# Values last in each attention visit, and gates behind the biases

## The chip, the cores and the metric

The kernel runs on one core of a Trainium2 chip. TensorE multiplies, VectorE (DVE), ScalarE (ACT) and GpSimd (POOL) work elementwise, SyncE (SP) issues most transfers; each engine runs its own instructions in order, and engines meet only through semaphores. The metric is the device time of one execution in microseconds, as a median over runs.

## The reference

One inference step of a hybrid backbone in f32: two layers over 1024 latent and 128 context tokens, width 1024. Every layer normalises, makes one input projection, feeds four mixers of 256 channels, multiplies each by its own gate path, and projects back:

```
h, gate = modulate(x, c, g, w_mod, b_mod)          # RMSNorm, scale and shift
parts = split_proj(h @ w_in)                       # 3584 columns
ya, yb = chunk_mlp(...) * silu(az), short_conv(...) * silu(bz)
yc = window_attn(cq, ck, cv, kc, vc, sink) * silu(cz)
yd = neighbourhood_attn(dq, dk, dv, kd, vd, rpb) * silu(dz)
x = x + gate * (concatenate([ya, yb, yc, yd]) @ w_out)
```

Both attention mixers have four heads of 64 channels. In C a block of 128 queries sees the blocks on both sides, itself and 128 cached keys; in D an 8 by 16 tile of the 16 by 64 grid sees 12 x 32 grid keys and the 128 cached ones, with a bias table. A block of context tokens sees only context tokens. Softmax over the keys, then the product with the values.

## The kernel before

**The stream of TensorE.** The input projection is 28 tiles of 128 columns, each in three chunks of 384 tokens. A chunk is one *step* (`STEPS`, 84 in a layer, numbered g from 0): 8 blocks of the inner dimension by three matmuls of 128x384 (high by high, high by low, low by high halves), 24 in all, at L919. Between steps TensorE pays a *visit* to the attention. A fixed table sets what it holds: a *pair* is two heads of one mixer for one block of 128 queries, 36 pairs in a layer, numbered p.

- `S_AT`: the **scores** of pair p (L939, two heads, contraction over 64 channels, so 64-row pieces of the array) in steps 12 to 29 (pairs 0 to 17), 31 to 39 and 43 to 51. SCALE and signs are folded in elsewhere.
- `T_AT` = that step + 2: the **turned probabilities** (L949), transposes of up to 4 blocks for each head by a product with the identity, 128x128.
- `V_AT` = that step + 3: the **values** product (L961), 64 output channels a head, so 64-column pieces of the array, into psum bank `BANK_O`, columns 0 to 127.

So a full visit of step g holds values of the pair of step g-3, turns of g-2 and scores of g, in this order. In the middle of a chunk (ahead of block k = 4) `misc(g)` puts in small pieces that use `BANK_O`, columns 128 up: turned values (L969), the mixing products of mixer A (L978), and for the modulation vectors `mod_sums` (L987, steps 15 and 16) and `mod_turn` (L995, steps 17 and 18). misc waits until all values issued so far have been gated; values of step g wait through `misc_free(g)` until the piece of step g has been read out of the bank.

**VectorE's step g**: gate of the pair whose values TensorE makes in this step (`gate_pair`, L1366, waits for `values_ready`); `take_part` (L1244: reads a z tile's chunk out of psum, frees its bank); for the scores of this step two `bias_unit` (sink copy L1335, and L1343, which adds a bias and takes the minimum); then rope (`ROPE_AT`: steps 6, 9, 15; L1222, L1224, L1227, with one product on GpSimd, L665), parts of the modulation sums (`multiply`, L1185, steps 6 to 13), two `norm_unit` (L1350, L1353, wait for the exponents), and `mods_at(g + 1)`, which reads the modulation piece of the next step's misc (copy L1198 for steps 15 and 16, L1207 for 17 and 18).

**ScalarE's step g**: takes or tanh of the chunk; `copy_probs` (L830) of the turned probabilities of this step, which waits until the values of the pair before are done, since it overwrites the buffer they read; the high half of the weights (L695) every third step; two exponents (L821), which wait for the biases; and the copy of the next step's turned values.

Of the kernel before, what the change touches and what calls it, by code (L numbers as in the profile page):

```python
# [96 lines left out]
GROUP_P = LT + 1  # L97
# [14 lines left out]
def build(nc, xT, cond, w_mod, b_mod, norm_g, final_g, w_tiles, w_sT, b_s, w_conv, sink, rpb,  # L112
          cckT, ccv, cdkT, cdv, ident_c, rope_c, band_c, row_c, col_c, yT, sckT, scvT, sdkT, sdvT):
    with ExitStack() as ctx:
# [411 lines left out]
        for layer in range(DEPTH):  # L526
          with nc.Block() as block:
# [383 lines left out]
            def _(pe):  # L911
# [41 lines left out]
                def values(p):  # L953

                    u = 2 * p
                    pe.wait_ge(copied, u + 2)
                    if p >= 1:
                        pe.wait_ge(gated, p)
                    for b in range(BLOCKS[u]):
                        for r in range(2):  # L960
                            last = nc.tensor.matmul(psum[64 * r:64 * r + 64, BANK_O, 0:P], unit_values(u + r)[b],  # L961
                                                    probT[:, r, b * P:(b + 1) * P], start=(b == 0),
                                                    stop=(b == BLOCKS[u] - 1), skip_group_check=True)
                    last.then_inc(values_ready, 1)
# [91 lines left out]
                for g, (n, c) in enumerate(STEPS):  # L1056
                    if c == 0:
                        pe.wait_ge(lo_ready, n + 1)
                    if n == 1 and c == 0:
                        pe.wait_ge(rstd_copied, NCH)  # L1060
                    if n >= 2:
                        pe.wait_ge(free[c], n - 1)
                    for k in order:
                        if k == 4:
                            misc(g)
                        if n == 0:
                            pe.wait_ge(h_odd if k % 2 else h_even, 4 * c + k // 2 + 1)
                        last = products(n, k, c, order)
                    last.then_inc(chunk_done, 1)

                    if g in V_AT:
                        p = V_AT[g]
                        if p == 0:
                            pe.wait_ge(cv_natural, 3)
                        misc_free(g)
                        if p == 2 * GROUP_P:
                            pe.wait_ge(cache0_in, 16)
                            pe.wait_ge(dv_natural, 6)
                        if p == 3 * GROUP_P:
                            pe.wait_ge(cache1_in, 16)  # L1080
                            pe.wait_ge(dv_natural, 12)
                        values(p)
                    if g in T_AT:
                        turn_probs(2 * T_AT[g])
                        turn_probs(2 * T_AT[g] + 1)
                    if g in S_AT:
                        p = S_AT[g]
                        if p == 0:
                            pe.wait_ge(layer_in, 16 * LAYER_IN)
                            pe.wait_ge(rope_ready, 2)  # L1090
                        if p == GROUP_P:
                            pe.wait_ge(rope_ready, 3)
                        if p == 2 * GROUP_P:
                            part_read(pe, NO["dk", 0])
                            for b in range(NCH):
                                part_read(pe, NO["dq", 0], b)
                        if p == 3 * GROUP_P:
                            part_read(pe, NO["dk", 1])
                            for b in range(NCH):
                                part_read(pe, NO["dq", 1], b)  # L1100
                        scores(p)

                order = Y_ORDER
                for f in range(KT):
# [21 lines left out]
            def _(dve):  # L1126
# [248 lines left out]
                                                ALU.subtract).then_inc(y_low_v, 1)  # L1375

                for g, (n, c) in enumerate(STEPS):
                    if g in V_AT:
                        gate_pair(V_AT[g])
                    take_part(n, c)  # L1380
                    if g in S_AT:
                        p = S_AT[g]
                        if p == 0:
                            dve.wait_ge(layer_in, 16 * LAYER_IN)
                            settle()
                            tell(nc.vector.tensor_scalar(sinks[:, :], sinks[:, :], -1.0, None, ALU.mult))
                            settle()
                        bias_unit(2 * p)
                        bias_unit(2 * p + 1)
                    if g in ROPE_AT:  # L1390
                        rope(ROPE_AT[g])
                    if g in MOD_AT:
                        multiply(MOD_AT.index(g))
                    if 52 <= g < 56:
                        normalise(g - 52)
                    if g in S_AT:
                        norm_unit(2 * S_AT[g])
                        norm_unit(2 * S_AT[g] + 1)
                    mods_at(g + 1)
                    if g + 1 in MIX_AT:  # L1400
                        read_mix(MIX_AT[g + 1])
                    if g >= OUT_0 - 3:
                        y_low(g - (OUT_0 - 3))
# [183 lines left out]
```

## Time and profile before

| | |
|---|---|
| median of 3 runs | 1307.63 us (1305.5 to 1308.05) |
| profiled execution, its own time | 1307.76 us |
| its span, first to last instruction | 1305.9 us |
| mean granted clock of TensorE | 0.964 |
| TensorE busy | 1205.3 us, 92% |
| VectorE, ScalarE, GpSimd busy | 50%, 33%, 26% |

Matmuls overlap in the pipeline, so the starts of the rows are a better measure than their durations: projection matmuls start 0.17 us apart and are listed with 0.33. In a timeline a group of like instructions in a row stands as one row with its count; one f32 matmul of values or scores is two records there, one turn is one. The granted clock is 1.00 at 2.4 GHz and 0.50 at 1.2 GHz.

### The profile page before, as it was taken

The page shows a single profiled execution, that of the slowest core. Times are in us where ns is not written, and L with a number is a line of the kernel's source. Part 1 is how long each engine was busy: PE and PEld are TensorE (multiplying, and loading weights), DVE is VectorE, ACT ScalarE, POOL GpSimd, SP SyncE. Part 2 cuts the span into 40 slices and gives each one's busy share as a digit, 9 for nine tenths or more (in the row PEclk, how much of TensorE's full clock was granted, in tenths as well). Part 3 has the DMA queues.
Part 4 walks back from the last instruction along what each step waited for, and adds up shares of the span by engine and source line. Part 5 has one row for each costly group of instructions (what it writes and reads, how often), then busy time and mean ns, then how long its engine had stood idle before and what let it go on. Part 6 is the DMA issues. An engine that isn't in the chain of part 4 may idle for free. (4 is left out here: it accounts for less than half of the span.)

```text
span 1305.9 us, 19971 instructions
## 1 busy us (share of the span) xinstructions
PE 1205.3 (92%) x8010; PEld 1109.7 (85%) x8010; DVE 648.1 (50%) x1310; ACT 430.2 (33%) x908; POOL 338.5 (26%) x222
## 2 busy tenths in 40 slices
PE   2589799999999999999958889999999999999993
PEld 0389698988888999999958878898888899999993
DVE  3667744444254532397667674444424444225225
ACT  3351344545354111221136233544434411123110
POOL 0243131034250212341123313102424112134110
PEclk9799999999999999999969999999999999999997
DMA  8714111021120111345342421102112000121213
GB/s 346 275 57 158 38 43 36 17 66 55 57 70 17 33 49 33 133 138 177 101 177 93 127 70 41 38 17 66 56 46 80 19 33 33 49 101 43 95 53 145
DMA packets 35948, 107.12 MB, mean 82 GB/s; under 512 B 5264, under 2 KB 14608, under 8 KB 34576
## 3 DMA queue, kind: packets, MB, share of 16 engines
q1 hardware_dynamic: 34128, 105.06, 23.1%
q8 instruction: 64, 1.05, 0.3%
q10 hardware_dynamic: 1728, 0.79, 0.2%
q14 instruction: 28, 0.23, 0.1%
HBM read 90.88 MB, written 14.94 MB: 81 GB/s over the span
## 5 line engine op out<-in xcount | busy, mean ns | idle before, releaser
L919 PE MATMUL psum<-h_hi,w_hi 128*128 128x384 f32 x1728 | 599.6, 347 | 35.5 <-POOL h_lo L653 16.4
L919 PE MATMUL psum<-h_hi,w_lo 128*128 128x384 f32 x1728 | 582.8, 337 | 0.0
L919 PE MATMUL psum<-h_lo,w_hi 128*128 128x384 f32 x1728 | 582.5, 337 | 0.0
L919 PEld LDWEIGHTS psum<-h_hi,w_hi 128*128 128x128 f32 x1728 | 327.7, 190 | 69.8 <-issue 23.7
L633 POOL TENSOR_TENSOR w_lo<-w_raw,w_hi 128x1024 fp32r<-128x1024 f32 x72 | 180.7, 2510 | 722.8 <-ACT w_hi L695 722.8
L919 PEld LDWEIGHTS psum<-h_lo,w_hi 128*128 128x128 f32 x1728 | 328.0, 190 | 0.0
L919 PEld LDWEIGHTS psum<-h_hi,w_lo 128*128 128x128 f32 x1728 | 327.5, 190 | 0.0
L695 ACT CAST w_hi<-w_raw 128x1024 fp32r<-128x1024 f32 x72 | 75.8, 1053 | 243.3 <-PE psum L919 234.5
L821 ACT ACTIVATE prob<-prob,stat 128x512 f32<-128x512 f32 (+2 forms) x144 | 96.8, 674 | 87.9 <-DVE stat L1343 87.5
L1366 DVE SCALAR_TENSOR_TENSOR xy<-psum,xy 128x128 f32<-128x128 f32 x72 | 21.0, 292 | 175.9 <-PE psum L961 175.9
L1353 DVE TENSOR_SCALAR prob<-prob,stat 128x512 f32<-128x512 f32 (+1 forms) x144 | 103.0, 715 | 8.8
L830 ACT COPY probT<-psum 128x512 f32<-128x512 f32 (+1 forms) x144 | 70.8, 543 | 77.8 <-PE psum L949 77.7
L1185 DVE SCALAR_TENSOR_TENSOR slots<-slots,silu 128x1024 f32<-128x1024 f32 x56 | 82.7, 1517 | 4.2 <-DMA slots<-in_w_mod 1.7
L961 PE MATMUL psum<-probT,slots 128*64 128x128 f32 x896 | 71.1, 285 | 11.5 <-DVE slots L1198 8.3
L961 PEld LDWEIGHTS psum<-probT,slots 128*64 128x64 f32 x896 | 49.5, 138 | 29.7 <-issue 20.3
L1343 DVE CUSTOM_DVE_ANT_0 prob<-psum,table 128x512 f32<-128x512 f32 (+1 forms) x72 | 43.7, 645 | 61.6 <-PE psum L939 61.6
L643 POOL TENSOR_TENSOR table<-row_mask,table 128x384 f32<-128x384 f32 x48 | 40.4, 841 | 129.6 <-DMA table<-in_rpb 129.5
L949 PE MATMUL psum<-ident,prob 128*128 128x128 f32 x512 | 73.1, 284 | 0.0
L1422 DVE SCALAR_TENSOR_TENSOR xy<-psum,mod,slots 128x384 f32<-128x384 f32 (+1 forms) x64 | 31.6, 514 | 81.2 <-PE psum L919 79.5
L782 ACT ACTIVATE slots<-psum 128x384 f32<-128x384 f32 x60 | 28.7, 488 | 119.4 <-PE psum L919 119.4
L949 PEld LDWEIGHTS psum<-ident,prob 128*128 128x128 f32 x512 | 56.7, 144 | 11.8 <-issue 11.6
L811 ACT ACTIVATE slots<-psum 128x384 f32<-128x384 f32 x48 | 23.6, 491 | 119.8 <-PE psum L919 119.8
(105 smaller groups left out, 968.0 us busy)
## 6 DMA issues: line engine op xcount, KB each, us to landing
w_raw<-in_w_tiles SPq DMA_DIRECT2D x72, 512.0 KB, 3.3
slots<-in_w_mod SPq DMA_DIRECT2D x32, 512.0 KB, 4.3
x_kept<-xy SPq DMA_DIRECT2D x16, 576.0 KB, 8.0
table<-in_rpb SPq DMA_DIRECT2D x48, 192.0 KB, 2.5
slots<-x_kept SPq DMA_DIRECT2D x16, 576.0 KB, 4.2
slots<-in_w_mod SPq DMA_DIRECT2D x8, 1024.0 KB, 7.3
xy<-in_xT SPq DMA_DIRECT2D x8, 576.0 KB, 7.1
out_yT<-slots SPq DMA_DIRECT2D x8, 576.0 KB, 3.2
```

Of the source, the lines that this page charges most:

```text
L633: nc.gpsimd.tensor_tensor(w_lo[:, n % 2], raw_of(n), w_hi[:, n % 2], ALU.subtract).then_inc(lo_ready, 1)
L643: own(nc.gpsimd.tensor_tensor(tab, rows, tab, ALU.subtract))
L695: nc.scalar.copy(w_hi[:, n % 2], w_raw[:, b]).then_inc(hi_ready, 1)
L821: nc.scalar.activation(row, row, ACT.Exp, scale=-1.0, bias=stat[:, u % 4, 0:1], accum_out=stat[:, u % 4, 1:2]).then_inc(expd, 1)
L830: nc.scalar.copy(probT[:, u % 2, 0:n * P], psum[:, BANK_T + u % 2, 0:n * P]).then_inc(copied, 1)
L919: last = nc.tensor.matmul(psum[:, bank, 0:CH], w[:, n % 2, k, :], h[:, k, cols_of(c)], start=(k == order[0] and w is w_hi and h is h_hi), ...
L949: last = nc.tensor.transpose(psum[:, BANK_T + u % 2, b * P:(b + 1) * P], prob[:, u % PROBS, b * P:(b + 1) * P], ident[:, :])
L961: last = nc.tensor.matmul(psum[64 * r:64 * r + 64, BANK_O, 0:P], unit_values(u + r)[b], probT[:, r, b * P:(b + 1) * P], start=(b == 0), st ...
L1185: ins = nc.vector.scalar_tensor_tensor(mod_part[cnd], mod_rows[g % 2], silu[:, k, cnd:cnd + 1], mod_part[cnd], ALU.mult, ALU.add)
L1343: nc.vector.tensor_tensor_reduce(out=row[:, 0:width], in0=psum[:, BANK_S + r, 0:width], in1=bias, scale=1.0, scalar=first, op0=ALU.add, op ...
L1353: nc.vector.tensor_scalar(row, row, stat[:, u % 4, 2:3], None, ALU.mult).then_inc(normed, 1)
L1422: last = nc.vector.scalar_tensor_tensor(xy[:, f, cols], psum[:, c, at], mod[:, 2 * KT + f, cnd:cnd + 1], x_new[:, f % 2, cols], ALU.mult, ...
```

## The change

In TensorE's visit the block for values moves behind turns and scores: turns, scores, values. In VectorE's step the gate moves behind the two biases. Where a step has no scores, the gate follows the take of the chunk.

```diff
@@ TensorE, after the products of step g
-                    if g in V_AT:
-                        p = V_AT[g]
-                        if p == 0:
-                            pe.wait_ge(cv_natural, 3)
-                        misc_free(g)
...
-                        values(p)
                     if g in T_AT:
                         turn_probs(2 * T_AT[g])
                         turn_probs(2 * T_AT[g] + 1)
...
                         scores(p)
+                    if g in V_AT:
+                        p = V_AT[g]
+                        if p == 0:
+                            pe.wait_ge(cv_natural, 3)
+                        misc_free(g)
...
+                        values(p)
@@ VectorE, step g
-                    if g in V_AT:
-                        gate_pair(V_AT[g])
                     take_part(n, c)
                     if g in S_AT:
...
                         bias_unit(2 * p)
                         bias_unit(2 * p + 1)
+                    if g in V_AT:
+                        gate_pair(V_AT[g])
                     if g in ROPE_AT:
                         rope(ROPE_AT[g])
```

TensorE, layer 0, the visit of step 34 (mixer D; L961 values, L949 turns, L939 scores against cached and grid keys, L919 projections). Before:

```order
L919 MATMUL psum<-h_hi,w_lo 128x384
L961 MATMUL psum<-probT,slots 64x128 x8
L949 MATMUL psum<-ident,prob 128x128 x8
L939 MATMUL psum<-ck_d,slots 128x128 x2
L939 MATMUL psum<-slots 128x384 x2
L919 MATMUL psum<-h_hi,w_hi 128x384
```

After:

```order
L919 MATMUL psum<-h_hi,w_lo 128x384
L949 MATMUL psum<-ident,prob 128x128 x8
L939 MATMUL psum<-ck_d,slots 128x128 x2
L939 MATMUL psum<-slots 128x384 x2
L961 MATMUL psum<-probT,slots 64x128 x8
L919 MATMUL psum<-h_hi,w_hi 128x384
```

Values moved from the front of the visit to its end; the turns now follow a projection, scores stand before values, and values before a projection.

TensorE, layer 0, the visit of step 15 (mixer C, the first with values). Before:

```order
L961 MATMUL psum<-probT,slots 64x128 x2
L961 MATMUL psum<-probT,cv_c 64x128 x2
L961 MATMUL psum<-probT,slots 64x128 x2
L949 MATMUL psum<-ident,prob 128x128 x8
L939 MATMUL psum<-slots 128x128 x6
L939 MATMUL psum<-ck_c,slots 128x128 x2
```

After:

```order
L949 MATMUL psum<-ident,prob 128x128 x8
L939 MATMUL psum<-slots 128x128 x6
L939 MATMUL psum<-ck_c,slots 128x128 x2
L961 MATMUL psum<-probT,slots 64x128 x2
L961 MATMUL psum<-probT,cv_c 64x128 x2
L961 MATMUL psum<-probT,slots 64x128 x2
```

The wait for the copy L1198, which stands ahead of L961, now has the turns and scores in front of it and not behind it.

VectorE, layer 0, from the copy L1198 at the end of step 14 through step 15 to the third rope (L1366 the gate, L1244 the take, L1335 and L1343 the biases, L1222 the rope's shuffle). Before:

```order
L1198 COPY slots<-psum 128x256
L1366 SCALAR_TENSOR_TENSOR xy<-psum,xy 128x128
L1244 SCALAR_TENSOR_TENSOR xy<-slots,psum 128x384
L1335 COPY prob<-sinks 128x1
L1343 ISA prob,stat<-psum,w_raw,sinks 128x512
L1343 ISA stat 128x1
L1335 COPY prob<-sinks 128x1
L1343 ISA prob,stat<-psum,w_raw,sinks 128x512
L1343 ISA stat 128x1
L1222 STREAM_SHUFFLE slots<-slots 128x1024
```

After:

```order
L1198 COPY slots<-psum 128x256
L1244 SCALAR_TENSOR_TENSOR xy<-slots,psum 128x384
L1335 COPY prob<-sinks 128x1
L1343 ISA prob,stat<-psum,w_raw,sinks 128x512
L1343 ISA stat 128x1
L1335 COPY prob<-sinks 128x1
L1343 ISA prob,stat<-psum,w_raw,sinks 128x512
L1343 ISA stat 128x1
L1366 SCALAR_TENSOR_TENSOR xy<-psum,xy 128x128
L1222 STREAM_SHUFFLE slots<-slots 128x1024
```

The gate went from the head of the step to between the biases and the rope. The order on the other engines and in the queues is the same.

## Rows read from the trace of the kernel before

**Rows 1.** The page's first part: busy us, share of the span, instructions.
```profile
PE 1205.3 (92%) x8010; PEld 1109.7 (85%) x8010; DVE 648.1 (50%) x1310; ACT 430.2 (33%) x908; POOL 338.5 (26%) x222
```
**Rows 2.** TensorE's waits: waiting line, releaser, us in total, times, longest us.
```profile
PE psum L961 <- DVE slots L1198: 8.3, 2, 4.2
...
PE psum L961 <- issue: 3.2, 2, 1.6
```
**Rows 3.** Timeline of TensorE, steps 15 and 16, layer 0: start, duration, work [idle before].
```profile
145.17 0.34 PE L919 MATMUL psum<-h_hi,w_lo 128*128 128x384 f32 x1
...
147.11 0.44 PE L961 MATMUL psum<-probT,slots 128*64 128x128 f32 x4 [1.61 <-issue]
...
148.94 0.94 PE L939 MATMUL psum<-slots 64*128 64x128 f32 x12
...
150.03 0.44 PE L919 MATMUL psum<-h_hi,w_hi 128*128 128x384 f32 x1
...
154.93 0.34 PE L919 MATMUL psum<-h_hi,w_lo 128*128 128x384 f32 x1
...
159.42 1.12 PE L961 MATMUL psum<-probT,slots 128*64 128x128 f32 x8 [4.16 <-DVE slots L1198]
...
164.86 0.45 PE L919 MATMUL psum<-h_hi,w_hi 128*128 128x384 f32 x1
```
**Rows 4.** Timeline of VectorE, step 15, layer 0; then the page's group of the gates.
```profile
146.59 0.42 DVE L1198 COPY slots<-psum 128x256 f32<-128x256 f32 x1
...
150.13 0.15 DVE L1335 COPY prob<-sinks 128x1 f32<-128x1 f32 x1 [1.36 <-PE psum L939]
...
151.61 1.35 DVE L1222 STREAM_SHUFFLE slots<-slots 128x1024 f32<-128x1024 f32 x1
...
158.95 0.42 DVE L1198 COPY slots<-psum 128x256 f32<-128x256 f32 x1
...
L1366 DVE SCALAR_TENSOR_TENSOR xy<-psum,xy 128x128 f32<-128x128 f32 x72 | 21.0, 292 | 175.9 <-PE psum L961 175.9
```
**Rows 5.** Timeline of TensorE, steps 33 and 34, and 42 (values alone), layer 0.
```profile
283.43 0.34 PE L919 MATMUL psum<-h_hi,w_lo 128*128 128x384 f32 x1
283.61 1.04 PE L949 MATMUL psum<-ident,prob 128*128 128x128 f32 x8
284.57 0.49 PE L939 MATMUL psum<-ck_d,slots 64*128 64x128 f32 x4
...
285.64 0.44 PE L919 MATMUL psum<-h_hi,w_hi 128*128 128x384 f32 x1
...
289.74 0.34 PE L919 MATMUL psum<-h_hi,w_lo 128*128 128x384 f32 x1
290.00 1.09 PE L961 MATMUL psum<-probT,slots 128*64 128x128 f32 x16
291.03 1.09 PE L949 MATMUL psum<-ident,prob 128*128 128x128 f32 x8
...
293.12 0.44 PE L919 MATMUL psum<-h_hi,w_hi 128*128 128x384 f32 x1
...
347.98 0.44 PE L961 MATMUL psum<-probT,slots 128*64 128x128 f32 x4
348.35 0.45 PE L919 MATMUL psum<-h_hi,w_hi 128*128 128x384 f32 x1
```
**Rows 6.** A wait; then stretches: length, five engines' busy time, PEclk, DMA, GB/s.
```profile
125.58 0.44 PE L919 MATMUL psum<-h_hi,w_hi 128*128 128x384 f32 x1 [2.62 <-DVE xy L1244]
...
127.00:128.00 1.00, 1.00 (x5) 1.00 (x4) 1.00 (x1) 0.00 (x0) 0.00 (x0) 0.50 1.02 410
...
160.00:162.00 2.00, 2.00 (x17) 1.67 (x14) 0.55 (x2) 0.00 (x0) 0.00 (x0) 0.50 0.00 0
```
**Rows 7.** Timeline of TensorE, step 16, layer 1.
```profile
782.88 1.12 PE L961 MATMUL psum<-probT,slots 128*64 128x128 f32 x8 [4.11 <-DVE slots L1198]
...
788.70 0.58 PE L919 MATMUL psum<-h_hi,w_hi 128*128 128x384 f32 x1
```

More of the change, by code:

```diff
@@ L1069, in _ @@
                     last.then_inc(chunk_done, 1)
-                    if g in V_AT:
-                        p = V_AT[g]
-                        if p == 0:
-                            pe.wait_ge(cv_natural, 3)
-                        misc_free(g)
[L1076 to L1081, printed above, removed]
-                        values(p)
                     if g in T_AT:
@@ L1101, in _ @@
                         scores(p)
+                    if g in V_AT:
[3 more added lines that the diff above has]
+                        misc_free(g)
+                        if p == 2 * GROUP_P:
+                            pe.wait_ge(cache0_in, 16)
+                            pe.wait_ge(dv_natural, 6)
+                        if p == 3 * GROUP_P:
+                            pe.wait_ge(cache1_in, 16)
+                            pe.wait_ge(dv_natural, 12)
+                        values(p)
                 order = Y_ORDER
```

## The prediction

> **What bounds the kernel now.** I read the page's busy shares first: TensorE is busy 92% of the span [rows 1] and every other engine half of it or less, so only what TensorE waits for, or loses between its own instructions, can move the end. The list of TensorE's waits comes next. Two of its entries belong to the values product, L961: 8.3 us in 2 waits released by the VectorE copy L1198, and 3.2 us in 2 waits put down to "issue" [rows 2]. There are two layers, so each is one wait a layer. The timeline puts them in the visits of steps 15 and 16, the first two that hold values. There I read TensorE and VectorE side by side [rows 3, 4]. Last, visits without any wait show what the order itself costs [rows 5].
>
> All starts below are of matmuls; I measure a visit from the start of the last projection matmul ahead of it to the start of the first one behind it.
>
> **Step 15.** The last projection matmul starts at 145.17. Values must wait for the copy L1198, 146.59 to 147.01, which reads the psum bank that values write into; they start at 147.11, scores at 148.94, projections at 150.03 [rows 3, 4]. The visit is 4.86 us. After the change turns and scores stand in front. Turns start 0.18 behind a projection (283.43 to 283.61), eight turned blocks up to scores are 0.96 (to 284.57) [rows 5], scores of this size 1.09 (148.94 to 150.03) [rows 3]. Values of 4 records take 0.37 up to what follows (347.98 to 348.35) and of 16 records 1.03 (290.00 to 291.03), 0.055 a record, so the 12 of step 15 take 0.81 [rows 5]. Values could start at 145.17 + 0.18 + 0.96 + 1.09 = 147.40, behind the end of the copy, so nothing waits; with 0.81 the visit is 3.04 us. Gain **1.82 us**, next projections at 148.21.
>
> **Step 16.** Here values wait for a second copy L1198, at 158.95, the last item of VectorE's step 15: gate, take, two biases, the third rope (shuffle at 151.61, a product, a wait for GpSimd's product, a sum), two normalisations, copy [rows 4]. TensorE starts its last projection at 154.93 and values only at 159.42, after 4.16 us idle; its clock is then at 0.50 (1.2 GHz), and projections start again at 164.86 [rows 3, 6]. What becomes of VectorE's step 15: the first bias starts 1.19 behind scores (148.94 to 150.13), and scores will start at 146.31, so at 147.50; the take, by then done straight behind the copy of 147.01, makes it 147.55 at the latest. Biases last 1.48 up to the shuffle (150.13 to 151.61); now the gate follows them, 0.29 [rows 4]. Shuffle at 147.55 + 1.48 + 0.29 = 149.32, **2.3 us earlier**. From the shuffle to the copy nothing changes its length, since GpSimd's product, the only thing waited for, is itself started by the shuffle; exponents are ready before the rope is. So values can start at 159.42 - 2.3 = 157.1. TensorE would be there at 148.21 + 4.90 (the projections of step 16, 150.03 to 154.93) + 0.18 + 0.96 + 1.09 = 155.34. It still waits 1.7 us, but turns and scores are done by then. Full values are 1.03: projections at 158.1 instead of 164.86, **6.7 us** for the two visits. In layer 1 values start at 782.88 and projections at 788.70 [rows 7]: 782.88 - 2.3 + 1.03 = 781.6, gain **7.1 us**. Together 13.8.
>
> **The clock in that remaining wait** is the one place where I choose. After 1.61 us idle in step 15 the pace stayed that of full speed (scores 1.09); after 4.16 us it was 0.50; after 2.62 us at 125.58 it was 0.50 from 127 on [rows 3, 6]. 1.7 us is nearest to 1.61, so I take full speed. If it fell, values would take twice their 1.03, and the projections behind them run at half speed for some 3 us, which loses half of that: about 2.5 us a layer.
>
> **All other full visits** (values, turns and scores) are steps 17 to 29, 31, 34 to 39 and 46 to 51: 26 a layer, 52 in all. Before: 289.74 to 293.12, 3.38 us. The same visit without values is 2.21 us (283.43 to 285.64) [rows 5]. The difference of 1.17 is 0.14 more than the 1.03 of values. Values between scores and projections: 0.37 for 4 records before a projection and 1.03 for 16 before turns lie on the one line of 0.055 a record that step 15's 12 records before turns (0.81, 147.11 to 147.92 in the same timeline) also meet, so what stands behind values makes no difference. After: 2.21 + 1.03 = 3.24, gain 0.14 each, 52 x 0.14 = **7.3 us**. The unknown is scores directly before values, which the trace never has; I give it what scores before a projection cost. The bounds: the extra that values pay behind a projection over turns (289.74 to 290.00 is 0.26, against 0.18) is 0.08 for a switch; one such less or one more is 52 x 0.08 = 4.2 us either way. Visits with values and turns alone keep two changes of shape and visits with values and scores three: nothing for them.
>
> The rows show turns (128x128 like the projections) 0.18 behind a projection and values (128x64) 0.26 behind it [rows 5]. The Trainium skill, "TensorEngine Tiling (Array Packing)", section Key Properties, says that a change of tiling mode drains the engine. By that rule a full visit has four changes before and three after, and the gain per visit is that one change; if the mode did not matter the term would be zero and the whole gain the 13.8 us. The trace agrees with the rule in this pair.
>
> **Costs I set at nothing.** ScalarE's copies of turned probabilities wait for values of the same visit and so begin about 1.7 us later; they are needed by the next visit's values, and the exponents behind them by turns two visits on, a whole visit of cover. Gates fall behind two biases: in a full visit at about 0.18 + 0.96 + 1.19 + 1.48 = 3.8 us, done at 4.1; the first to ask for them is the misc piece in the middle of the next chunk, at 3.24 + 2.1 = 5.3 us (half of a chunk's 4.2): 1.2 us of cover. The take moves ahead of the gate, and its bank is asked for three steps later. GpSimd's and SyncE's queues keep their order; ScalarE's high halves of weights come 1 to 2 us later, two steps before they are needed.
>
> **Sum.** 13.8 + 7.3 = 21.1 us. Behind step 16 the list of waits has nothing for TensorE up to the mixing products, so nothing takes it back. The profiled execution took 1307.76 us (span 1305.9); its like after the change is 1286.7. The median of the runs shown is 1307.63, 0.1 lower, so the forecast is **1287 us**.
>
> **Rivals.**
> 1. The clock falls in the remaining wait of step 16: 2 x 2.5 us back, 1292 us. For it: 2.62 us of idle time were enough once. Against it: 1.61 us were not [rows 3, 6]. Chance 0.20.
> 2. The switch from scores to values. A dearer one, or an order that saves none: the 7 us go, 1294 us, chance 0.12. A cheaper one: 4.2 us more, 1283 us, chance 0.08.
> 3. Slower: gates come late. If VectorE reaches the gate more than 1.2 us later than reckoned, the pieces in the middle of the next chunk wait for it. There are 20 such steps a layer (16 to 18, 25 to 30, 37 to 42, 47 to 51), 40 in all. The gain is used up at 21.1 / 40 = 0.53 us each, so from a gate 1.7 us late on; at 2.0 us late it is 1286.7 + 40 x 0.8 = 1319 us. Against it: take, biases, gate and normalisations are some 4 of the 7.5 us of a step. Chance 0.04.
> 4. VectorE's chain of step 15 is held by something else (exponents, GpSimd), and values of step 16 start as late as now. Turns and scores then run inside the wait, but the clock falls: values take 1.9 us, projections start at 161.4 and lose another 1.5 us at half speed, so 2.0 of 6.7 us a layer are left: 1307.8 - 4.0 - 7.3 = 1296.5 us. Chance 0.08. That nothing moves by 0.2%: 0.03.
>
> A change of 0.2% (2.6 us) is about what a measurement of this kernel can tell from none. The forecast itself has 0.45. The range of 1282 to 1297 takes in cases 1, 2 and 4. Faster 0.93, same 0.03, slower 0.04.
>
> **What would show it.** Right: no idle time before values in step 15; in step 16 about 1.7 us, with the clock at full speed behind it; full visits of 3.24 us with 1.07 from scores to values; 2.3 us less between the first copy L1198 and the shuffle of the third rope. Wrong: waits of the middle pieces on the gate L1366, a full visit at 3.38 us or above, or a clock of 0.50 behind step 16.

## The result and the profile after

| | before | after |
|---|---|---|
| median of runs | 1307.84 us (4 runs, 1305.5 to 1314.39) | 1289.81 us (4 runs, 1286.4 to 1291.82) |
| profiled execution | 1307.76 us | 1286.4 us |
| its span | 1305.9 us | 1284.6 us |
| mean granted clock | 0.964 | 0.970 |

The ratio after to before is 0.9857, 95% interval 0.9827 to 0.9887: 1.4% faster. The forecast was 1287 us, range 1282 to 1297.

The page of after, first part (busy us, share, instructions), to be read against [rows 1]:

```profile
PE 1192.1 (93%) x8010; PEld 1110.6 (86%) x8010; DVE 657.7 (51%) x1310; ACT 423.0 (33%) x908; POOL 341.4 (27%) x222
```

No work was taken out: TensorE has the same 8010 instructions. TensorE's waits in after (waiting line, releaser, us in total, times, longest), as in [rows 2]:

```profile
PE psum L961 <- DVE slots L1198: 3.3, 2, 1.6
```

Values waited 8.3 + 3.2 us before [rows 2] and wait 3.3 us now. The entry put down to "issue", step 15's, is gone. Steps 15 and 16 of layer 0, TensorE, as in [rows 3] (start, duration, work, idle before):

```profile
144.10 0.34 PE L919 MATMUL psum<-h_hi,w_lo 128*128 128x384 f32 x1
...
146.33 0.44 PE L961 MATMUL psum<-probT,slots 128*64 128x128 f32 x4
...
147.14 0.44 PE L919 MATMUL psum<-h_hi,w_hi 128*128 128x384 f32 x1
...
152.04 0.34 PE L919 MATMUL psum<-h_hi,w_lo 128*128 128x384 f32 x1
...
155.98 0.66 PE L961 MATMUL psum<-probT,slots 128*64 128x128 f32 x8 [1.64 <-DVE slots L1198]
...
157.01 0.44 PE L919 MATMUL psum<-h_hi,w_hi 128*128 128x384 f32 x1
```

Step 15's visit is 147.14 - 144.10 = 3.04 us, step 16's 157.01 - 152.04 = 4.97 us. From the last projection matmul ahead of step 15's visit to the first one behind step 16's, layer 0 takes 12.91 us where it took 164.86 - 145.17 = 19.69 [rows 3]: 6.78 us gained. In layer 1 the same stretch is 758.14 to 771.05:

```profile
758.14 0.34 PE L919 MATMUL psum<-h_hi,w_lo 128*128 128x384 f32 x1
...
770.03 0.66 PE L961 MATMUL psum<-probT,slots 128*64 128x128 f32 x8 [1.64 <-DVE slots L1198]
...
771.05 0.44 PE L919 MATMUL psum<-h_hi,w_hi 128*128 128x384 f32 x1
```

Before, this stretch started at 768.65 in the timeline of that layer and ended at 788.70 [rows 7], so 20.05 us became 12.91: 7.14 us. A full visit of after, step 34, against the one of [rows 5]:

```profile
279.56 0.34 PE L919 MATMUL psum<-h_hi,w_lo 128*128 128x384 f32 x1
...
281.02 0.81 PE L939 MATMUL psum<-slots 64*128 64x384 f32 x4
281.77 1.09 PE L961 MATMUL psum<-probT,slots 128*64 128x128 f32 x16
282.79 0.44 PE L919 MATMUL psum<-h_hi,w_hi 128*128 128x384 f32 x1
```

It is 3.23 us, 0.15 less than 3.38; values start 1.07 behind the start of scores (280.70). VectorE in step 15, as in [rows 4]:

```profile
145.56 0.42 DVE L1198 COPY slots<-psum 128x256 f32<-128x256 f32 x1
...
147.94 0.28 DVE L1366 SCALAR_TENSOR_TENSOR xy<-psum,xy 128x128 f32<-128x128 f32 x1
...
148.15 1.35 DVE L1222 STREAM_SHUFFLE slots<-slots 128x1024 f32<-128x1024 f32 x1
...
155.51 0.42 DVE L1198 COPY slots<-psum 128x256 f32<-128x256 f32 x1
```

From the first copy to the shuffle it is 2.59 us, where it was 151.61 - 146.59 = 5.02 [rows 4]: 2.43 us less.

**Where the 21.3 us of span went**, by how much earlier the same point of the program is reached:

| up to | earlier, us | gained in this part |
|---|---|---|
| last projection ahead of step 15's visit, layer 0 (145.17, 144.10) | 1.07 | 1.07, not forecast |
| behind step 16's visit (164.86, 157.01) | 7.85 | 6.78 |
| behind step 42's visit (348.35, 337.45) | 10.90 | 3.05: 2.99 in the 20 full visits, 0.06 in all the rest |
| ahead of step 15's visit, layer 1 (768.65, 758.14) | 10.51 | -0.39: 0.90 in six full visits, and 1.29 lost, 1.1 of it in step 13's visit (1.76 before, 2.86 after, both with a wait for the bias L1343) |
| behind step 16's visit (788.70, 771.05) | 17.65 | 7.14 |
| end of the span (1305.9, 1284.6) | 21.3 | 3.65: 3.90 in the 26 full visits, 0.25 lost elsewhere |

Pairs of numbers are the starts before and after of the same projection matmul. Step 42's visit itself, values alone, kept its length (0.64).

### The profile page after: what moved, and what is told of

Read it like the earlier page. It is cut to its first block and busy times, and to the rows that moved or that the text cites. A ratio compares the mean times of both kernels' runs of the same rounds, so it can differ in the third digit from the quotient of the medians.

```text
span 1284.6 us, 19971 instructions
## 1 busy us (share of the span) xinstructions
PE 1192.1 (93%) x8010; PEld 1110.6 (86%) x8010; DVE 657.7 (51%) x1310; ACT 423.0 (33%) x908; POOL 341.4 (27%) x222
## 5 line engine op out<-in xcount | busy, mean ns | idle before, releaser
L919 PE MATMUL psum<-h_hi,w_hi 128*128 128x384 f32 x1728 | 600.3, 347 | 33.4 <-POOL h_lo L653 16.2
L919 PE MATMUL psum<-h_hi,w_lo 128*128 128x384 f32 x1728 | 583.6, 338 | 0.0
L919 PE MATMUL psum<-h_lo,w_hi 128*128 128x384 f32 x1728 | 583.3, 338 | 0.0
L919 PEld LDWEIGHTS psum<-h_hi,w_hi 128*128 128x128 f32 x1728 | 328.2, 190 | 60.7 <-issue 22.1
L633 POOL TENSOR_TENSOR w_lo<-w_raw,w_hi 128x1024 fp32r<-128x1024 f32 x72 | 181.2, 2517 | 716.0 <-ACT w_hi L695 715.9
L919 PEld LDWEIGHTS psum<-h_lo,w_hi 128*128 128x128 f32 x1728 | 328.7, 190 | 0.0
L919 PEld LDWEIGHTS psum<-h_hi,w_lo 128*128 128x128 f32 x1728 | 328.3, 190 | 0.0
L1353 DVE TENSOR_SCALAR prob<-prob,stat 128x512 f32<-128x512 f32 (+1 forms) x144 | 114.9, 798 | 5.8
L830 ACT COPY probT<-psum 128x512 f32<-128x512 f32 (+1 forms) x144 | 70.7, 544 | 138.9 <-PE psum L961 138.9
L1343 DVE CUSTOM_DVE_ANT_0 prob<-psum,table 128x512 f32<-128x512 f32 (+1 forms) x72 | 43.7, 644 | 80.2 <-PE psum L939 79.7
L961 PE MATMUL psum<-probT,slots 128*64 128x128 f32 x896 | 69.6, 281 | 3.3 <-DVE slots L1198 3.3
L961 PEld LDWEIGHTS psum<-probT,slots 128*64 128x64 f32 x896 | 48.4, 136 | 23.3 <-issue 15.8
L949 PE MATMUL psum<-ident,prob 128*128 128x128 f32 x512 | 67.6, 272 | 0.0
L782 ACT ACTIVATE slots<-psum 128x384 f32<-128x384 f32 x60 | 28.7, 489 | 117.1 <-PE psum L919 117.1
L1350 DVE RECIPROCAL stat<-stat 128x1 f32<-128x1 f32 x144 | 23.0, 160 | 83.2 <-ACT prob L821 82.8
L939 PE MATMUL psum<-slots 64*128 64x128 f32 (+1 forms) x512 | 58.2, 341 | 4.9 <-DVE stat L1343 2.9
L949 PEld LDWEIGHTS psum<-ident,prob 128*128 128x128 f32 x512 | 60.4, 141 | 2.5
```

Of the source, the lines that this page charges most:

```text
L633: nc.gpsimd.tensor_tensor(w_lo[:, n % 2], raw_of(n), w_hi[:, n % 2], ALU.subtract).then_inc(lo_ready, 1)
L830: nc.scalar.copy(probT[:, u % 2, 0:n * P], psum[:, BANK_T + u % 2, 0:n * P]).then_inc(copied, 1)
L919: last = nc.tensor.matmul(psum[:, bank, 0:CH], w[:, n % 2, k, :], h[:, k, cols_of(c)], start=(k == order[0] and w is w_hi and h is h_hi), ...
L939: last = nc.tensor.matmul(psum[:, BANK_S + r, at:at + width], queries(u + r), src, start=True, stop=True, skip_group_check=True)
L949: last = nc.tensor.transpose(psum[:, BANK_T + u % 2, b * P:(b + 1) * P], prob[:, u % PROBS, b * P:(b + 1) * P], ident[:, :])
L1343: nc.vector.tensor_tensor_reduce(out=row[:, 0:width], in0=psum[:, BANK_S + r, 0:width], in1=bias, scale=1.0, scalar=first, op0=ALU.add, op ...
```

## The experiments

The first four ran on one chip beside 13 runs of the kernel before (median 1307.64 us), the next four beside 11 (1307.4), the last three beside 9 (1307.42). Each ratio is to the kernel before of its own group.

### Each half of the change alone

**e1: TensorE's part alone.** After, with the gate where it was:

```diff
                 for g, (n, c) in enumerate(STEPS):
+                    if g in V_AT:
+                        gate_pair(V_AT[g])
                     take_part(n, c)
...
-                    if g in V_AT:
-                        gate_pair(V_AT[g])
                     if g in ROPE_AT:
```

> The changed kernel with VectorE's order of before: gate first, then the take and the biases; TensorE keeps turns, scores, values. Theory (the wait of step 16 is VectorE's chain from the copy L1198 to the next copy): the gate now waits for the end of values at the end of the visit, and take and biases follow it, so the third rope's shuffle comes 1.2 us later than in the changed kernel; idle time before values in step 16 about 2.8 us, full visits stay 3.24 us, about 1289.5 us, and 1294 us if the clock falls in that longer wait. Rival (only TensorE's order counts, VectorE's is free): as the changed kernel, 1.6 us idle.

Measured: 1291.33 us (4 runs), ratio 0.9876 (0.9856 to 0.9896). TensorE in step 16, layer 0, and the stretch from 158 to 159 (length, busy time of PE, PEld, DVE, ACT and POOL, granted clock, DMA share, GB/s):

```profile
158.40 1.12 PE L961 MATMUL psum<-probT,slots 128*64 128x128 f32 x8 [2.87 <-DVE slots L1198]
...
160.31 0.69 PE L919 MATMUL psum<-h_hi,w_hi 128*128 128x384 f32 x1
...
158.00:159.00 1.00, 0.60 (x6) 0.60 (x8) 0.35 (x2) 0.00 (x0) 0.00 (x0) 0.50 0.00 0
```

VectorE now waits 1.29 us at the gate, since values are made last, and only then does take and biases:

```profile
146.74 0.42 DVE L1198 COPY slots<-psum 128x256 f32<-128x256 f32 x1
148.45 0.29 DVE L1366 SCALAR_TENSOR_TENSOR xy<-psum,xy 128x128 f32<-128x128 f32 x1 [1.29 <-PE psum L961]
...
150.59 1.35 DVE L1222 STREAM_SHUFFLE slots<-slots 128x1024 f32<-128x1024 f32 x1
```

Copy to shuffle is 3.85 us instead of 2.59, so the copy that values of step 16 wait for is 1.26 later, and TensorE's wait grows from 1.64 to 2.87. Visit 16 is 7.08 us in layer 0, where the clock fell, and 6.20 in layer 1, where it did not: 2.1 and 1.2 us more than in after. That is what moving the gate is worth when it stands beside the new order. The medians say as much (1291.33 against 1287.5 to 1289.81 for after), but their intervals overlap.

**e2: the gates alone.** Before, with the gate behind the biases (TensorE's order as before):

```diff
                 for g, (n, c) in enumerate(STEPS):
-                    if g in V_AT:
-                        gate_pair(V_AT[g])
                     take_part(n, c)
...
+                    if g in V_AT:
+                        gate_pair(V_AT[g])
                     if g in ROPE_AT:
```

> The kernel before with only VectorE's part of the change: gate behind the biases; TensorE keeps values, turns, scores. Theory: the shuffle of the third rope comes 0.3 us later than before, values of step 16 wait about 4.4 us with the clock at 0.50 behind it, full visits stay 3.38 us; the gate ends about 5.3 us after the last projection, 0.2 us ahead of the middle piece, so no new wait: 1308.5 us, no difference. Rival (the cover is smaller than reckoned): waits of L969 on the gate L1366 in some of 40 steps, 0.2 us each, up to 1316 us.

Measured: 1308.18 us (10 runs), ratio 1.0004 (0.9991 to 1.0018): nothing. The waits of step 16's values on the copy are there at full length:

```profile
PE psum L961 <- DVE slots L1198: 8.7, 2, 4.4
```

With values first, the gate's input is ready before the biases' is. Ahead of the biases the gate lies in a time in which VectorE waits for the scores anyway (1.36 us in [rows 4]); behind them it adds its 0.29 us to the chain, and values of step 16 wait 4.4 us instead of 4.2. The move pays only because TensorE now makes values last.

The wait in step 15 is less fixed than [rows 3] make it look. In layer 0 of e2, TensorE's order being that of before, visit 15 has no wait (3.19 us) and the wait put down to "issue" stands once in the list instead of twice; there TensorE had already waited 3.0 us in step 13, where the kernel before waited 1.4. So the 1.8 us that the change gains in step 15 need not be gained in full in every execution.

### Which order, and why

**e3: scores, turns, values**, and **e4: values, scores, turns.** The three blocks of TensorE's visit permuted: e3 in the kernel after, e4 in the kernel before.

```diff
@@ e3, TensorE's visit of after; values(p) stands behind it
-                    if g in T_AT:
-                        turn_probs(2 * T_AT[g])
-                        turn_probs(2 * T_AT[g] + 1)
                     if g in S_AT:
...
                         scores(p)
+                    if g in T_AT:
+                        turn_probs(2 * T_AT[g])
+                        turn_probs(2 * T_AT[g] + 1)
@@ e4, TensorE's visit of before
                         values(p)
-                    if g in T_AT:
-                        turn_probs(2 * T_AT[g])
-                        turn_probs(2 * T_AT[g] + 1)
...
                         scores(p)
+                    if g in T_AT:
+                        turn_probs(2 * T_AT[g])
+                        turn_probs(2 * T_AT[g] + 1)
```

> The changed kernel with scores ahead of turns in the visit: scores, turns, values. Values are still last and gates still behind the biases. Theory (a full visit pays for each change of shape of the array; this order has four like before, since scores stand behind a projection): step 16's wait stays short (about 1.7 us), but full visits go back to 3.38 us: 1286.7 + 7.3 = 1294 us. Rival (what saves time is that values stand last): full visits 3.24 us and 1287 us.

> The kernel before with turns last in the visit: values, scores, turns; gates first as before. Theory (changes of shape): turns stand before a projection of the same shape, three changes, full visits 3.24 us as in the changed kernel, while the waits of steps 15 and 16 (1.6 and 4.2 us, clock 0.50 behind the second) stay nearly as before, a little shorter since scores and so the rope come 1.0 us earlier in step 15 (3.2 us in step 16): about 1298 us. Rival (the saving comes from values at the end): full visits 3.38 us, 1305 us.

Measured: e3 1292.87 us (4 runs), ratio 0.9892 (0.9872 to 0.9912); e4 1297.21 us (4 runs), 0.9926 (0.9902 to 0.9949). A full visit of e3, then one of e4:

```profile
298.42 0.34 PE L919 MATMUL psum<-h_hi,w_lo 128*128 128x384 f32 x1
298.69 0.49 PE L939 MATMUL psum<-ck_d,slots 64*128 64x128 f32 x4
...
299.76 1.09 PE L949 MATMUL psum<-ident,prob 128*128 128x128 f32 x8
300.78 1.09 PE L961 MATMUL psum<-probT,slots 128*64 128x128 f32 x16
301.80 0.44 PE L919 MATMUL psum<-h_hi,w_hi 128*128 128x384 f32 x1
```

```profile
293.62 0.34 PE L919 MATMUL psum<-h_hi,w_lo 128*128 128x384 f32 x1
293.89 1.09 PE L961 MATMUL psum<-probT,slots 128*64 128x128 f32 x16
...
295.99 1.09 PE L949 MATMUL psum<-ident,prob 128*128 128x128 f32 x8
296.84 0.42 PE L919 MATMUL psum<-h_hi,w_hi 128*128 128x384 f32 x1
```

Four kinds of work stand in a visit, projections and turns with 128x128 pieces of the array, scores with 64x128, values with 128x64. Counted between neighbours, the pieces change four times in the kernel before and in e3, and three times in after and in e4. The visits are 3.38 and 3.38 us, 3.23 and 3.22 us. All 26 full visits of a layer, those of both layers alike, come to 81.94 us in the kernel before and in e3, 78.05 in after, and 77.40 in e4 if step 18's new wait (below) is left out. So two orders with values last differ by 0.15 a visit, and two with values first by 0.17: the gain per visit goes with the number of changes, not with where values stand. The Trainium skill, "TensorEngine Tiling (Array Packing)", section Key Properties, says that a change of tiling mode drains the engine; these four orders agree, at 0.15 to 0.17 us for one change more or less.

Step 16 tells the two terms apart. e3 has values last and 1.1 us of wait there: its longer visits bring TensorE 0.3 us later than in after, counted from the last projection ahead of visit 15, and the copy comes 0.2 earlier. e4 has the cheap visits and the old waits on the copy (8.0 us in 2), and one more:

```profile
PE psum L961 <- DVE mod L1207: 2.2, 2, 1.1
```

That entry was not expected: step 18's values, at the front of the visit, now wait for the read L1207. e4 gains 10.4 us by its medians and 11.7 by the spans of the two traces. The full visits are 9.1 of it, visit 15 is 1.46 shorter in each layer (3.40 us, with a wait of 0.3 instead of 1.6), visit 16 is 1.0 and 1.4 shorter (8.90 in both), and the new waits take 2.2 back: 12.2 in all, within half a microsecond of the spans. In e4 most of the wait of step 15 is gone too; that of step 16 is not.

### The same kernel again

**e5** and **e11** are the kernel after itself, beside the second and the third group.

> The changed kernel again, on the same chip as the next three, to see its spread: its four runs lay between 1286.4 and 1291.8 us. Theory: the wait of 1.6 us in step 16 keeps the clock at full speed in this trace too, and the spread comes from the stretches at 1.2 GHz behind other waits (step 13 and the border of the layers), whose length differs between runs; median 1286 to 1292 us. Rival: in some executions the clock falls behind step 16 (2.5 us a layer); then a trace with a longer time shows values of step 16 at half speed.

> The changed kernel again, as the measure for the two others on the same chip: between 1284 and 1292 us, full visits 3.24 us, 1.6 us of idle time in step 16 at full clock in both layers.

Measured: e5 1287.93 us (5 runs), ratio 0.9854 (0.9832 to 0.9876); e11 1287.5 us (4 runs), 0.9844 (0.9831 to 0.9857). e5's visits 15 and 16 are those of after (3.04, then 4.98 and 4.96 us, no stretch at 0.50 behind them). e11's are not, in one place. TensorE in layer 0, then one stretch:

```profile
151.47 0.34 PE L919 MATMUL psum<-h_hi,w_lo 128*128 128x384 f32 x1
...
155.46 0.86 PE L961 MATMUL psum<-probT,slots 128*64 128x128 f32 x8 [1.69 <-DVE slots L1198]
...
157.10 0.69 PE L919 MATMUL psum<-h_hi,w_hi 128*128 128x384 f32 x1
...
160.06 0.34 PE L919 MATMUL psum<-h_hi,w_lo 128*128 128x384 f32 x1
...
156.00:158.00 2.00, 2.00 (x15) 1.67 (x12) 1.66 (x7) 0.73 (x2) 0.00 (x0) 0.50 0.00 0
```

The granted clock, third from the end, is 0.50 from 156 to 158. The same stretch in after:

```profile
156.00:158.00 2.00, 2.00 (x22) 1.83 (x23) 2.00 (x8) 0.82 (x2) 0.00 (x0) 1.00 0.00 0
```

The wait is the same (1.69 against 1.64), but here the granted clock fell to 0.50. The visit is 157.10 - 151.47 = 5.63 us instead of 4.97, and the 12 projection matmuls behind it take 160.06 - 157.10 = 2.96 instead of 159.02 - 157.01 = 2.01: 0.66 + 0.95 = 1.6 us lost. Layer 1 of the same execution kept 1.00. So rival 1 is real, in some executions and not in others (one of the six visits 16 in the three traces of this kernel), at 1.6 us a layer and not 2.5.

### The price of a late gate

**e6.** After, with the gate moved to the end of VectorE's step:

```diff
-                    if g in V_AT:
-                        gate_pair(V_AT[g])
                     if g in ROPE_AT:
                         rope(ROPE_AT[g])
...
                         norm_unit(2 * S_AT[g] + 1)
+                    if g in V_AT:
+                        gate_pair(V_AT[g])
                     mods_at(g + 1)
```

> The changed kernel with the gate moved further back in VectorE's step, behind rope, modulation part and the two normalisations. It prices the rival on the slower side. Theory (1.2 us of cover, then one for one): the gate comes about 6.7 us after the last projection (7.7 where ScalarE has a high half of weights to make) and the middle piece asks for it at 5.3: 1.4 to 2.4 us of wait in 20 steps a layer, and in step 16 the piece waits for the whole rope, about 6 us: some 44 us a layer, 1375 us. Rival (the gate has far more cover): 1287 us.

Measured: 1403.58 us, one run, where 1375 was expected. TensorE's waits:

```profile
PE psum L969 <- DVE xy L1366: 32.1, 16, 3.5
PE psum L969 <- issue: 31.0, 14, 3.4
...
PE psum L987 <- issue: 12.7, 2, 6.5
...
PE psum L995 <- DVE xy L1366: 10.5, 4, 3.9
```

These are 86.3 us in 36 waits, about the 44 us a layer that were expected; after has none of them. The mechanism is rival 3's, at the pieces that it named. The other 31 of the 117 us over 1286.4 are in no wait, and the expectation left them out: behind many of these waits the clock is low, for example from 158 to 162:

```profile
158.00:162.00 4.00, 4.00 (x16) 3.74 (x13) 0.43 (x1) 0.00 (x0) 0.00 (x0) 0.50 0.00 0
```

By the mean clocks, 0.947 and 0.970, some 70 us more of this execution than of after stood at 0.50; half of that time lost would be 35 us, an estimate near the 31. A late gate thus cost a third more than its waits. In after the gate of step 15 ends at 147.94 + 0.28 = 148.22, and the middle piece of step 16 starts at 149.43: 1.2 us of cover. Over the 40 pieces of both layers the cover is 1.0 us (step 17) to 1.8, where 1.2 was reckoned.

### The wait that is left

Of step 16's 1.64 us the cause is the copy L1198 at the end of VectorE's step 15, behind rope and normalisations. Four kernels take it forward.

**e7.** The copy ahead of the rope:

```diff
+                    if g == 15:
+                        mods_at(16)
                     if g in ROPE_AT:
                         rope(ROPE_AT[g])
...
-                    mods_at(g + 1)
+                    if g != 15:
+                        mods_at(g + 1)
```

> The changed kernel with VectorE's copy L1198 for step 16 put ahead of the third rope (it then waits some 2 us for the sums in the middle of step 16). Theory (what is left of the wait in step 16 is the rope standing ahead of the copy): no idle time before values in step 16, full speed, 1.7 us a layer less: 3.4 us less than the changed kernel on the same chip. The rope ends 2 us later, and nothing of TensorE's asks for it before step 21. Rival (another wait takes its place, normalised probabilities for the turns of step 17): no gain.

Measured: 1293.21 us (6 runs), ratio 0.9889 (0.9868 to 0.991). That is 5.3 us above after in its group (1287.93), where 3.4 less was expected; the two intervals overlap at their edges (0.9868 and 0.9876). VectorE, then TensorE:

```profile
152.26 0.42 DVE L1198 COPY slots<-psum 128x256 f32<-128x256 f32 x1 [1.94 <-PE psum L987]
...
162.12 0.28 DVE L1366 SCALAR_TENSOR_TENSOR xy<-psum,xy 128x128 f32<-128x128 f32 x1
...
162.55 0.41 PE L995 MATMUL psum<-ident,slots 128*128 128x128 f32 x2 [2.78 <-DVE xy L1366]
```

Values of step 16 no longer wait. But the copy needs TensorE's piece in the middle of step 16, so VectorE idles 1.94 us ahead of it, the rope and all behind it end later, the gate of step 16 is late, and the small piece of step 17 waits 2.78 us for it (5.9 us in both layers by the list of waits, where the waits removed were 3.3). The wait moved one step on and grew, and in layer 1 the clock fell behind it: visit 17 took 4.12 us instead of 3.26. This execution, the slowest of the six, also has waits that lie ahead of the place of the edit (3.0 us in step 13 and 2.5 at the piece L987 of step 15, both in layer 0), so its trace prices only what is named here.

**e8.** The copy inside the rope, in the gap in which VectorE waits for GpSimd's product, and in steps 6 and 9 parts of the modulation sums in the same gap:

```diff
-                def rope(j):
+                def rope(j, between):
...
                     tell(nc.vector.tensor_tensor(swapped, swapped, sin_t, ALU.mult))
+                    between()
                     settle()
                     dve.wait_ge(cos_ready, j + 1)
...
-                        rope(ROPE_AT[g])
-                    if g in MOD_AT:
+                        rope(ROPE_AT[g], lambda: mods_at(16) if g == 15 else multiply(MOD_AT.index(g)))
+                    elif g in MOD_AT:
...
-                    mods_at(g + 1)
+                    if g != 15:
+                        mods_at(g + 1)
```

> The changed kernel with VectorE's idle time inside each rope (2.35 us, until GpSimd's product is there) filled: with that step's part of the modulation sums in steps 6 and 9, with the copy L1198 in step 15. Theory (VectorE is behind from step 6 on, and TensorE's waits in steps 12 to 14, 1.0 + 2.2 + 1.5 us a layer with a stretch at 1.2 GHz behind, are the same cause as those of steps 15 and 16): these waits go almost entirely, and the 1.7 us of step 16 too: 14 to 16 us less than the changed kernel, 1272 us. Rival (those waits come from the transfers of w_mod, not from VectorE's work): only the 3.4 us of step 16.

**e9.** Only the copy of step 15 in the gap:

```diff
                     tell(nc.vector.tensor_tensor(swapped, swapped, sin_t, ALU.mult))
+                    if between:
+                        between()
...
-                        rope(ROPE_AT[g])
+                        rope(ROPE_AT[g], (lambda: mods_at(16)) if g == 15 else None)
...
-                    mods_at(g + 1)
+                    if g != 15:
+                        mods_at(g + 1)
```

> The changed kernel with only this: in step 15 VectorE's copy L1198 stands inside the third rope, between its product and its sum, where VectorE waits for GpSimd. Nothing is put into the ropes of steps 6 and 9. Theory (the last wait of step 16 goes at no cost to the rope, unlike where the copy stood ahead of the rope): values of step 16 start without a wait, 1.65 us a layer; the middle piece of step 17 waits 0.4 to 0.6 us for the gate, so about 2.4 us less than the changed kernel on the same chip. Rival (the wait only moves to the middle piece in full): no difference, or a loss as with the copy ahead of the rope.

**e10.** e9, and in step 16 the gate ahead of take and biases, as in the kernel before:

```diff
+                    if g == 16:
+                        gate_pair(V_AT[g])
                     take_part(n, c)
...
-                    if g in V_AT:
+                    if g in V_AT and g != 16:
                         gate_pair(V_AT[g])
```

> The kernel with the copy L1198 inside the third rope, and in step 16 alone the gate ahead of the take and the biases, since VectorE comes to that step after the values are done. Theory: the 0.4 to 0.6 us of wait of the middle piece of step 17 go too: 3.3 us less than the changed kernel on the same chip, the lowest time of all. Rival: the biases of step 16 come 0.2 us later and something else of step 17 waits for them instead: no less than without this.

| | median, us | ratio (95%) | against after in its group |
|---|---|---|---|
| e8 | 1286.66 (4 runs) | 0.9839 (0.9817 to 0.9861) | -1.3, intervals overlap |
| e9 | 1285.56 (5 runs) | 0.9836 (0.9819 to 0.9853) | -1.9, intervals overlap |
| e10 | 1282.79 (4 runs) | 0.9812 (0.9799 to 0.9826) | -4.7, intervals apart |

e10: VectorE, then TensorE, in steps 15 to 17 of layer 0 (two lines are added ahead of them in the code, so the sum is L1229 and the gate L1368):

```profile
151.06 0.42 DVE L1198 COPY slots<-psum 128x256 f32<-128x256 f32 x1
153.32 1.22 DVE L1229 TENSOR_TENSOR slots<-slots 128x1024 f32<-128x1024 f32 x1 [1.83 <-POOL slots L665]
...
152.28 0.34 PE L919 MATMUL psum<-h_hi,w_lo 128*128 128x384 f32 x1
...
155.53 0.44 PE L919 MATMUL psum<-h_hi,w_hi 128*128 128x384 f32 x1
```

The copy costs VectorE nothing, since it lies in a gap that is there anyway (2.35 us in after, 0.42 and 1.83 here). Visit 16 is 155.53 - 152.28 = 3.25 us, and the pieces of steps 16 and 17 don't wait; in e9 the piece of step 17 still waited for the gate (0.8 us in both layers). The 4.7 us are more than the 2 x 1.64 of the wait. The traces of e10 and e11, of one chip, have spans of 1280.4 and 1285.5, 5.1 us apart: visit 16 is 2.4 and 1.7 us shorter in the two layers, and the projections behind it in layer 0, which e11 ran in part at half speed, 0.9. So in these two executions the wait and the clock behind it account for the whole difference; what differs elsewhere, under 1 us each, cancels out. e10 is the fastest kernel here, 1.9% below the kernel before.

e8's other half, at steps 6 and 9, gave nothing, and the forecast of 1272 us was far off:

```profile
104.66 1.42 DVE L1182 TENSOR_SCALAR slots<-slots,silu 128x1024 f32<-128x1024 f32 x2 [12.67 <-DMA slots<-in_w_mod]
...
118.10 6.52 DVE L1185 SCALAR_TENSOR_TENSOR slots<-slots,silu 128x1024 f32<-128x1024 f32 x2
```

In step 6 the sums put into the gap waited for a transfer, and held the rope with them: its sum starts at 106.17, where after has it at 99.08, and TensorE's scores of step 12 waited 4.7 us a layer for it. In step 9 two of them took 6.52 us, where two elsewhere take 2.48.

## Why the prediction held, step by step

- **Step 15.** Forecast 3.04 us without a wait; measured 3.04, no wait, in both layers. The durations came from other visits of the trace before, except that of the scores, which is step 15's own.
- **VectorE's chain.** Forecast 2.3 us off it up to the third rope; measured 2.43. e1 shows that 1.26 of it hang on the gate's move.
- **Step 16.** Forecast 1.7 us of wait and 6.7 and 7.1 us gained in the two layers; measured 1.64 in both, 6.78 and 7.14. The reason was right too: only the wait behind the copy was left, and the third rope with what follows kept its length (148.15 to 155.51 is 7.36, before 151.61 to 158.95 is 7.34). Rival 4, a chain held elsewhere, did not come.
- **The clock.** Full speed was the choice, by the nearest of three waits, and in after and e5 it held. e11 shows the other outcome at an equal wait, 1.6 us a layer, so that after's trace shows none of it is in part luck. The price of 2.5 was mis-sized: half speed ended within the 12 projections behind the visit (0.95 us lost, where 1.5 was taken), and values themselves lost 0.66 and not 1.03. That the case is one of executions, not of kernels, was not in the prediction. It may be one reason why the median (1289.81, later 1287.93 and 1287.5) lies above the profiled 1286.4, which the sum had at 1286.7, but none of the slower executions of this kernel was traced. Between its three traces (after, e5, e11) the largest difference is in the stretch from the end of the last attention visit of layer 0 to visit 15 of layer 1, 341.3, 339.2 and 341.1 us, where waits on the take L1244 and the bias L1343 vary from one execution to the next; it was not followed further.
- **Full visits.** Forecast 3.24, measured 3.23 to 3.24 in mixer D, on which the forecast was made, and 3.26 in mixer C, where it was 3.41 before; 7.3 us forecast, 81.94 - 78.05 = 3.89 in each layer measured, 7.8 together. e3 and e4 confirm the reason. The forecast drew its 0.14 from one pair of visits, as what values cost more when they stand first; the four orders show it to be the price of one change of shape, as the prediction held beside it. The one unknown, scores directly before values, cost what scores before a projection cost.
- **Gates' cover.** About 1.2 us forecast, 1.0 to 1.8 measured, no wait on L1366 in after; e6 shows the cost of losing it.
- **Costs set at nothing.** ScalarE's copies of turned probabilities now wait 138.9 us in all for values, where they waited 77.7 us for turns, and TensorE's list of waits has no entry for them: they cost nothing, as forecast.
- **What was missed.** 1.07 us of the 21.3 were already there ahead of step 15, where the change does nothing. The two terms that were forecast at 21.1 came to 13.9 + 7.8 = 21.7; the rest gave those 1.07 and took some 1.5 back, most of it in step 13 of layer 1. That 21.3 lies so near 21.1 is in part luck; the terms themselves are right to 0.5 us.

## What to carry to other kernels

Put the block whose input comes last behind those that are ready, and then look at the engine that feeds it: its own order must follow, or it waits for the block that has moved (e1). Count the changes of the array's shape in each order of a repeated visit; one fewer in 52 visits was over a third of this gain. A wait that remains is best met in a gap that another wait leaves open (e10), not ahead of work that others need (e7).

## What the runs showed of the hardware

**An equal wait, two clocks.** Behind an idle time of 1.64 us the granted clock stayed at 1.00 (after), behind 1.69 us it fell to 0.50 (e11, layer 0); behind some 2.9 us it fell in layer 0 of e1 and stayed in layer 1 (1.00 from 774 to 776).

The length of a single wait does not decide it; what does is open.

**VectorE and GpSimd lengthen each other's operations.** Kernel after, step 9, VectorE and then GpSimd:

```profile
114.27 1.22 DVE L1224 TENSOR_TENSOR slots<-slots,table 128x1024 f32<-128x1024 f32 x1
117.86 3.39 DVE L1227 TENSOR_TENSOR slots<-slots 128x1024 f32<-128x1024 f32 x1 [2.37 <-POOL slots L665]
...
114.31 3.44 POOL L665 TENSOR_TENSOR slots<-slots,table 128x1024 f32<-128x1024 f32 x1 [5.90 <-DVE slots L1222]
117.77 2.40 POOL L633 TENSOR_TENSOR w_lo<-w_raw,w_hi 128x1024 fp32r<-128x1024 f32 x1
```

Whichever starts second takes longer by about what is left of the first: GpSimd's product, 0.04 us behind L1224, is listed with 3.44 us, 1.04 more than the 2.40 of GpSimd alone; VectorE's sum, 0.09 us behind GpSimd's L633, with 3.39 instead of 1.23. e8's pair of 6.52 us ran beside two GpSimd operations (116.81 and 120.22, 3.44 and 3.31 us). The Trainium skill, "SBUF — State Buffer", section "SBUF: two separate sides", says that a GpSimd operation that reads SBUF and a VectorE operation with two SBUF inputs lock each other out for their whole length; the rows agree: 1.22 - 0.04 = 1.18 for the 1.04, and 1.23 + 2.40 - 0.09 = 3.54 for the 3.39. Other places of the traces serve as the test. In after, the rope's sum of step 15 had no GpSimd operation beside it and took 1.23 us. In the kernel before, the pair of sum and L633 met in either order in step 9: in layer 0 the sum began first (119.12, 1.23 us) and GpSimd's L633 at 119.47 took 3.12; in layer 1 L633 began first (742.30, 2.40 us) and the sum at 742.45 took 3.33.
